# A ring of three PSUM banks for attention's turned tiles, one output bank copied by ScalarE, and another order of VectorE's rounds

## The reference

```python
for l in range(DEPTH):                       # DEPTH = 2
    proj = rms_norm(x, norm1[l]) @ w_in[l]
    o_a = causal_block_attention(q_a, k_a, v_a, 96 ** -0.5)            # "A"
    o_b = sliding_window_attention(q_b, k_b, v_b, swa_sinks[l], ...)   # "B"
    o_c = dsa_attention(q_c, k_c, v_c, qi, ki, c_w, top_k, ...)        # "C"
    o_d = causal_block_attention(..., log_f_cum=cum)                   # "D"
    x = x + concatenate([o_a, o_b, o_c, o_d]) @ w_out[l]
    x = x + square(relu(rms_norm(x, norm2[l]) @ w_up[l])) @ w_down[l]
```

## Time and profile before

| | |
|---|---|
| median of 3 runs | 1879.53 us (1877.53 to 1884.22) |
| the profiled execution | 1878.71 us, span 1876.9 us |
| mean granted TensorE clock | 0.985 |
| TensorE matmul, busy | 1815.8 us (97%) |
| VectorE, busy | 933.3 us (50%) |
| ScalarE, busy | 650.0 us (35%) |
| GpSimd, busy | 731.0 us (39%) |
| the chain that ended last | TensorE 81%, VectorE 8%, "issue" 6%, ScalarE 3%, GpSimd 2% |

### The profile page before, as it was taken

How to read it: one execution, slowest core, us unless ns; L and a number is a source line. 1 busy time by engine, 2 the same in 40 slices (tenths; PEclk the granted TensorE clock), 3 DMA queues, 4 the chain that set the end, 5 groups by cost and what they waited for, 6 DMA issues and landing times.

```text
span 1876.9 us, 22981 instructions
## 1 busy us (share of the span) xinstructions
PE 1815.8 (97%) x9055; PEld 1472.2 (78%) x9057; DVE 933.3 (50%) x1556; ACT 650.0 (35%) x1182; POOL 731.0 (39%) x328
## 2 busy tenths in 40 slices
PE   8999889999999999998999999999999999999997
PEld 7678558888888886785578888888788988888786
DVE  4668871614142336688725544628532124339374
ACT  4534452312221245344523121222434443443212
POOL 3232343444454433332534445445343333235342
PEclk9999899999999999998999999999899999999999
DMA  7225002222322333120014344342332222322211
GB/s 227 68 68 167 3 24 68 90 90 92 111 89 89 89 86 104 62 74 1 24 55 164 119 157 149 101 175 90 95 124 90 68 68 96 108 68 90 90 68 45
DMA packets 104448, 171.01 MB, mean 91 GB/s; under 512 B 21615, under 2 KB 39431, under 8 KB 103208
## 3 DMA queue, kind: packets, MB, share of 16 engines
q1 hardware_dynamic: 103320, 169.79, 27.6%
q10 hardware_dynamic: 1040, 0.00, 0.0%
HBM read 166.56 MB, written 7.93 MB: 93 GB/s over the span
## 4 chain that ended last, share of the span: by engine, by line
PE 81%; DVE 8%; issue 6%; ACT 3%; POOL 2%; DMA 0%; SPq 0%; DVEq 0%; POOLq 0%; ACTq 0%
PE G L2044 23%; PE G L2045 23%; PE G L2046 23%; POOL w_lo L1286 2%; PE S L2330 2%; DVE neg_max L1916 1%; PE S L1057 1%; DVE select L1880 1%; ACT prob L1513 1%; DVE work L1716 1%; PE S L1031 1%; PE G L2366 1%; DVE top L1715 1%; PE S L1042 1%; PE G L2347 1%
## 5 line engine op out<-in xcount | busy, mean ns | idle before, releaser
L1286 POOL TENSOR_TENSOR w_lo<-raw,w_hi 128x1024 fp32r<-128x1024 f32 (+2 forms) x268 | 661.0, 2487 | 989.4 <-ACT w_hi L1332 677.1
L2044 PE MATMUL G<-h_hi,w_hi 128*128 128x512 f32 x896 | 356.6, 398 | 4.0 <-POOL w_lo L1286 2.1
L1332 ACT ACTIVATE w_hi<-raw 128x2048 fp32r<-128x2048 f32 (+1 forms) x94 | 178.8, 1902 | 499.6 <-PE G L2046 499.6
L2046 PE MATMUL G<-h_hi,w_lo 128*128 128x512 f32 x896 | 350.4, 391 | 0.0
L2045 PE MATMUL G<-h_lo,w_hi 128*128 128x512 f32 x896 | 350.0, 391 | 0.0
L2044 PE MATMUL G<-w_hi,h_hi 128*128 128x512 f32 (+2 forms) x704 | 278.4, 395 | 5.7 <-issue 2.0
L2046 PE MATMUL G<-w_hi,h_lo 128*128 128x512 f32 (+2 forms) x704 | 268.7, 382 | 0.0
L2045 PE MATMUL G<-w_lo,h_hi 128*128 128x512 f32 (+2 forms) x704 | 268.3, 381 | 0.0
L2045 PE MATMUL G<-w_lo,u_hi 128*128 128x512 f32 x512 | 202.0, 394 | 0.0
L2044 PEld LDWEIGHTS G<-h_hi,w_hi 128*128 128x128 f32 x896 | 168.7, 188 | 42.3 <-issue 4.4
L2044 PE MATMUL G<-w_hi,u_hi 128*128 128x512 f32 x512 | 200.8, 392 | 0.0
(11 more groups left out here) (317 smaller groups left out, 2241.1 us busy)
## 6 DMA issues: line engine op xcount, KB each, us to landing
raw<-in_w_in_dram SPq DMA_DIRECT2D x40, 1024.0 KB, 5.2
raw<-in_w_up_dram SPq DMA_DIRECT2D x32, 1024.0 KB, 5.2
raw<-in_w_down_dram SPq DMA_DIRECT2D x32, 1024.0 KB, 5.0
raw<-in_w_out_dram SPq DMA_DIRECT2D x12, 1024.0 KB, 5.0
w_ada<-in_w_ada_dram SPq DMA_DIRECT2D x4, 3072.0 KB, 12.1
skew_scratch<-line_scratch SPq DMA_DIRECT2D x1, 4608.0 KB
raw<-in_w_in_dram SPq DMA_DIRECT2D x8, 512.0 KB, 4.4
raw<-in_w_in_dram SPq DMA_DIRECT2D x4, 832.0 KB, 6.7
```

Of the source, the lines that this page charges most:

```text
L1286: ins = pool.tensor_tensor(w_lo[:, c % SPLIT_SLOTS, part, 0:n], raw[:, c % RAW_SLOTS, part, 0:n], w_hi[:, c % SPLIT_SLOTS, part, 0:n].bitc ...
L1332: act.activation(w_hi[:, c % SPLIT_SLOTS, :, 0:n], raw[:, c % RAW_SLOTS, :, 0:n], ACT.Copy).then_inc(high_ready, 1)
L2044: pe.matmul(dst, a_hi, b_hi, start=first, stop=False)
L2046: return pe.matmul(dst, a_lo, b_hi, start=False, stop=last)
```

## The change

- The banks: turns go round banks 0, 1 and 2 of G; a turn waits for the turn three before it. All outputs go to bank 3, and an output waits until the one before it has been copied away.
- The takers: who copies a turn is now set by the unit or head (number n or e of it, even VectorE, odd ScalarE), no longer by the turn's number. The list TAKER keeps it, and the waits count in it.
- Output copies (L1944) go from VectorE to ScalarE, behind its copy of turned probabilities.
- Units of the next pair: one at step 0 of a pair, two at step 1, one at step 2; for C one at step 0 and one at step 1. Before, two at step 1 and two at step 2, for C both at step 1.
- VectorE's copy of a unit moves from the front of its step to the end of the step before, behind the rounds.
- Rounds: 36 instead of 30 are placed beside the projections, none of them in the last of those steps; 12 are left for the stage, two at steps 3, 7, 11 and 15 and one at 4, 8, 12 and 16.
- At the end, VectorE's splits get waits of their own for turns and outputs, and TensorE no longer waits for the output before the last ahead of the projection.

Cut to what is spoken of (left out are lines where only the bank's number changes, and VectorE's old `take_output`):

```diff
@@ -81,30 +81,51 @@
 def next_qk(i):
     p = ITEMS[min(i, NI - 1)][0] + 1
-    if i % TT not in (1, 2) or p == len(PAIRS):
+    if p == len(PAIRS):
         return p, ()
-    return p, range(2) if i % TT == 1 else range(2, qk_units(p))
+    return p, ((0,), (1, 2), (3,), ())[i % TT] if qk_units(p) == 4 else ((0,), (1,), (), ())[i % TT]
 def number_turns():
-    qk = {(0, n): n for n in range(qk_units(0))}
-    at, pt = qk_units(0), {}
+    qk, pt, taker = {}, {}, []
+    def add(places, key, who):
+        places[key] = len(taker)
+        taker.append(who)
+    for n in range(qk_units(0)):
+        add(qk, (0, n), n % 2)
     for i in range(NI + 1):
         p, units_now = next_qk(i)
         for n in units_now:
-            qk[p, n] = at
-            at += 1
+            add(qk, (p, n), n % 2)
         if i:
             for e in range(2):
-                pt[i - 1, e] = at
-                at += 1
-    return qk, pt, at
...
+QK_NO, PT_NO, TAKER = number_turns()
+LAYER_TURNS = len(TAKER)
+TURN_BANKS = 3
+def taken_by(who, no):
+    return TAKER[:no + 1].count(who)
+def turn_bank(no):
+    return no if no < 4 else (no - 4) % TURN_BANKS
+def bank_before(no):
+    return no - TURN_BANKS if no >= 4 + TURN_BANKS else turn_bank(no)
 MIX_ORDER = (0, 1, 2, 3, 4, 6, 7, 5)
@@ -179,9 +200,16 @@
 LAYER_SC = NB + NI
 LAYER_OV = NI
-EARLY_ROUNDS = 2 * ROUNDS
-EARLY_STEPS = side_steps(1, NS + 1)
-assert LAYER_TURNS % 2 == 0
+EARLY_ROUNDS = 9 * ROUNDS // 4
+EARLY_STEPS = side_steps(1, AT["M",]) - 1
+def late_rounds(i):
+    return {3: 2, 0: 1 if i else 0}.get(i % TT, 0)
+assert EARLY_ROUNDS + sum(late_rounds(i) for i in range(4 * TT + 2)) >= 3 * ROUNDS
...
@@ -1517,9 +1545,9 @@
                 def take_qk(p, units_now):
                     for n in units_now:
                         m, (what, _, at), no = head_width(p), qk_places(p)[n], QK_NO[p, n]
-                        if no % 2:
+                        if TAKER[no]:
                             act.wait_ge(turn_filled, turns + (no + 1))
-                            act.activation(qkT[0:m, p % 2, at, :], G[0:m, no if no < 4 else 1, :], ACT.Copy,
+                            act.activation(qkT[0:m, p % 2, at, :], G[0:m, turn_bank(no), :], ACT.Copy,
                                            scale=score_scale(p) if what == "q" else 1.0).then_inc(odd_drained, 1)
                 def take_probs(i):
@@ -1527,7 +1555,15 @@
                     act.wait_ge(turn_filled, turns + (PT_NO[i, 1] + 1))
                     if i >= 2:
                         act.wait_ge(o_filled, item0 + (i - 1))
-                    act.activation(probT[:, i % 2, 1, 0:width], G[:, 1, 0:width], ACT.Copy).then_inc(odd_drained, 1)
+                    act.activation(probT[:, i % 2, 1, 0:width], G[:, turn_bank(PT_NO[i, 1]), 0:width], ACT.Copy
+                                   ).then_inc(odd_drained, 1)
+                def take_output(i):
+                    p, qt = ITEMS[i]
+                    g, hp = PAIRS[p]
+                    q = slice(P * qt, P * qt + P)
+                    act.wait_ge(o_filled, item0 + (i + 1))
+                    act.activation(mixed(g, hp)[:, q], G[:, TT - 1, 0:P], ACT.Copy).then_inc(o_drained, 1)
                 def part_high(part):
                     c = MID_PIECE
@@ -1549,6 +1585,8 @@
                         exponentials(i + 1)
                     if i:
                         take_probs(i - 1)
+                    if i > 1:
+                        take_output(i - 2)
                     if i in MID_HIGH:
                         part_high(MID_HIGH[i])
                     for k in EARLY_SPLITS.get(i, ()):
@@ -1559,6 +1597,7 @@
                 act.wait_ge(o_drained, item0 + (5 * TT + PAIR_CREDIT))
                 for k in MIX_ORDER[HALF_K:KT - 1]:
                     high_mix(k)
+                take_output(NI - 1)
                 act.wait_ge(o_drained, item0 + (NI + PAIR_CREDIT))
                 high_mix(MIX_ORDER[KT - 1])
                 ahead(OUT_JOB, 0)
@@ -1719,16 +1758,16 @@
                     left = work[:, 0:P * (qt + 1)]
                     step.done(dve.tensor_scalar(chosen(qt), left, TAKEN * 0.9, NEG, ALU.is_gt, ALU.mult))
-                rounds = iter(range(EARLY_ROUNDS + ROUNDS))
+                rounds = iter(range(3 * ROUNDS))
                 round_steps = itertools.count()
                 def top_rounds(count=None):
                     if count is None:
                         k = next(round_steps)
+                        if k >= EARLY_STEPS:
+                            return
                         count = (k + 1) * EARLY_ROUNDS // EARLY_STEPS - k * EARLY_ROUNDS // EARLY_STEPS
-                        if k == EARLY_STEPS - 1:
-                            return
                     for r in itertools.islice(rounds, count):
                         top_round(1 + r // ROUNDS, r % ROUNDS)
                         if r % ROUNDS == ROUNDS - 1:
...
@@ -2289,29 +2324,27 @@
                 pe.wait_ge(bank_drained, unit + (TT * PROJ_JOBS - 3 + UNITS_CREDIT))
                 pe.wait_ge(even_taken, evens + (EVEN[AT["F",], "s"] + 1))
-                def turn_free(no):
-                    pe.wait_ge(odd_drained if no % 2 else even_drained, halves + (no // 2 + 2))
-                def turn_bank(no):
-                    return G[:, no if no < 4 else no % 2, :]
-                def turns_taken(no):
-                    pe.wait_ge(even_drained, halves + (no // 2 + 1 + PAIR_CREDIT))
-                    pe.wait_ge(odd_drained, halves + ((no + 1) // 2 + PAIR_CREDIT))
+                def unit_taken(no):
+                    who = TAKER[no]
+                    pe.wait_ge(odd_drained if who else even_drained,
+                               l * taken_by(who, LAYER_TURNS) + taken_by(who, no) + PAIR_CREDIT)
+                def units_taken(no):
+                    pe.wait_ge(even_drained, l * taken_by(0, LAYER_TURNS) + taken_by(0, no) + PAIR_CREDIT)
+                    pe.wait_ge(odd_drained, l * taken_by(1, LAYER_TURNS) + taken_by(1, no) + PAIR_CREDIT)
                 def give_qk(p, units_now):
                     for n in units_now:
                         (what, e, _), no = qk_places(p)[n], QK_NO[p, n]
                         if no >= 4:
-                            turn_free(no)
+                            unit_taken(bank_before(no))
                         elif no:
                             pe.wait_ge(bank_drained, unit + (TT * (PROJ_JOBS - 1) + no + 1 + UNITS_CREDIT))
                         for t in range(TT):
                             src = head_rows(p, what, e, t)
-                            ins = pe.transpose(turn_bank(no)[0:src.shape[1], P * t:P * t + P], src, ident)
+                            ins = pe.transpose(G[0:src.shape[1], turn_bank(no), P * t:P * t + P], src, ident)
                         ins.then_inc(turn_filled, 1)
                 def give_scores(i):
...
@@ -2358,11 +2391,11 @@
                     p = ITEMS[i][0]
                     tiles = key_tiles(i)
-                    turns_taken(PT_NO[i, 1])
-                    pe.wait_ge(o_drained, item0 + (i + 1))
+                    units_taken(PT_NO[i, 1])
+                    pe.wait_ge(o_drained, item0 + (i + PAIR_CREDIT))
                     for b, kb in enumerate(tiles):
-                        for e, dst in enumerate(output_bank(i)):
+                        for e, dst in enumerate(output_places()):
                             ins = pe.matmul(dst, values(p, e, kb), probT[:, i % 2, e, P * b:P * b + P],
                                             start=b == 0, stop=b == len(tiles) - 1)
                     ins.then_inc(o_filled, 1)
@@ -2384,8 +2417,6 @@
                         give_output(i - 2)
-                pe.wait_ge(o_drained, item0 + (NI - 1 + PAIR_CREDIT))
                 def last_bank_free(pos):
                     if pos == 3 * HALF_K - 1:
                         pe.wait_ge(o_drained, item0 + (NI + PAIR_CREDIT))
```

More of the change, by code:

```diff
@@ L1164, in mixed, with output_places @@
             return {"D": mixT_da, "A": mixT_da, "B": mixT_bc, "C": mixT_bc}[g][:, n + (2 if g in "AC" else 0), :]
-        def output_bank(i):
-            return [G[HD * e:HD * e + HD, 2 + i % 2, 0:P] for e in range(2)]
+        def output_places():
+            return [G[HD * e:HD * e + HD, TT - 1, 0:P] for e in range(2)]
         def select_at(qt):
@@ L1956, in _ @@
                         take_probs(i - 1)
[L1957 to L1960 removed]
+                    top_rounds(late_rounds(i))
+                    take_qk(*next_qk(i + 1))
                     if i + 1 < NI:
@@ L1963, in _ @@
                     if i == NI - 1:
+                        dve.wait_ge(turn_filled, turns + (PT_NO[NI - 2, 1] + 1))
                         split_mix(0, 2)
@@ L2126, in _ @@
                 unit, tr, item0, score0 = l * LAYER_UNITS, l * LAYER_TR, l * NI, l * LAYER_SC + NB
-                number, turns, halves = l * LAYER_PIECES, l * LAYER_TURNS, l * HALF_TURNS
+                number = l * LAYER_PIECES
```

33 lines of the change are left out of this document (14 added, 19 removed).

## The result

The changed kernel takes 1853.38 us (median of 4 runs, 1851.58 to 1854.34) against 1880.03 us (1877.53 to 1884.22) for the kernel before: a ratio of 0.9869, 95% interval 0.9851 to 0.9888. The profiled execution took 1854.13 us, its span is 1852.3 us, the mean granted clock 0.994; that is 24.6 us less in span than before. The forecast was 1856.5 us. One of the six executions of the version with two turn banks took 9632.1 us, for which no trace shows a reason; its median is given without it.

The account below looks back on a forecast made before the run. The two attention stages bound it, TensorE busy 77 to 81 of 90 to 92 us and waiting for banks and copies. Layers -13.9 and -12.2 make -26.1, hand-overs +3, so -23: 1856.5 us, range 1850 to 1872.

Parts of the forecast that it names:

- Start: First scores to the maxima of item 3 in each attention stage: -6.0 us in the first layer, -5.8 in the second.
- Periods: Each attention stage's four-item periods: 14.35, 14.8, 12.85, 12.4 us; first layer -3.85, -0.5, -1.05, -1.6, second layer's fourth -0.1.
- End: Last widest maxima to the output projection's first matmul: 17.38 to 15.7 us, -1.7 a layer, VectorE's splits beginning earlier.
- Hand-overs: Allowance for hand-overs that the pass leaves out: 48 items at 0.06 us give back 3 us.
- Rounds moved: Beside the projections, VectorE gets 8.5 us more a layer: +0.8 a layer, bounds 0 and 8.5 less 0.4.
- The wait that is added: One output bank: output(i-2) waits for ScalarE's copy of output(i-3); no cost beyond output(1)'s start at 3.2, plus 0.45 us a layer.
- The rival in which the single bank serialises: Slower rival: each output waits out the queued exponentials, mean 1.02 us, 48 cost 49 us, time 1905 us; chance 0.07.
- The clock falls all the same: Rival: short pauses still lower the clock in the stages, 4.6 us a layer, 9.2 in all, time 1865.7 us; chance 0.14.
- VectorE's three rounds keep the period: Rival: VectorE's queue at item 3 keeps periods at 15.3, 15.3, 13.9, 14.0 and 12.5; 6.8 us lost, 1863.3; chance 0.15.
- Moved rounds in full: Rival: the rounds moved beside the projections cost in full, 7.7 us more in each layer, time 1872 us; chance 0.07.

Follow-up runs that it names:

- the second experiment: The kernel before with only the new placing of rounds (36 beside the projections, 12 in the stage): 1890.99 us, ratio 1.0084.
- the first experiment: The changed kernel with the rounds placed as before (30 beside the projections, 18 in the stage): 1855.83 us, ratio 0.9891 against the kernel before.

## Why the prediction was right, point by point

**Parts and placing in one table.** Stages of layer 1 / layer 2 in us:

| | rounds as before | 36/12, two in a row | 36/12, singly |
|---|---|---|---|
| banks and order before | 92.08 / 90.32 | 94.17 / 94.13 | 87.70 / 87.67 |
| banks and order changed | 81.22 / 80.58 | 78.15 / 78.16 | 74.40 / 74.41 |

The ring, ScalarE's output copies, the unit copies at the end of the step and the three steps bring 13 to 16 us a stage in the last two columns and 10 to 11 in the first. The changed placing of the rounds is worth 2 to 3 us with the new banks and costs 2 to 4 with the old: the pair at step 3 is harmful in both rows, by 6.5 with the old banks and 3.75 with the new. I hadn't costed this coupling on its own. The clock is part of these numbers: its mean in the two stages is 0.89 and 0.94, 0.95 and 0.95, 0.94 and 0.94 in the first row, and 0.94 and 0.98, then 1.00 four times in the second. With the rounds singly, 8.7 of the 13.3 us between the rows are busy time of TensorE (77.43 against 68.78 us). How much of a gain is a shorter wait, and how much the clock that stays up behind it, these runs don't separate; only where both cells have 1.00, as with 78.15 and 74.40, is it the waits alone.

**Start**: right. 7.25 us in both layers, clock 1.00; the working had 7.25. Both parts of the change are in it: with the rounds back it is 11.28 with the same banks, with the rounds moved but the old banks and order 9.36, and with two turn banks and all else new 8.33.

**Periods**: the first 14.37 for a forecast of 14.35; the second 14.94 for 14.8; the third 13.00 for 12.85. The fourth is mis-sized: 12.87 for 12.4. Between 242.08 and 250.94 VectorE has no pause there, and behind the third round comes the mark of C's last tile:

```profile
249.26 0.43 DVE L1759 TENSOR_SCALAR select<-work 128x512 bf16<-128x512 f32 x1
...
249.81 0.94 DVE L1955 TENSOR_REDUCE neg_max<-S 128x2 f32<-128x768 f32 x1
```

My pass for that period named no mark. But with single rounds the same mark stands in the same place (245.01, behind the third round) and the period is 11.91. So the mark isn't enough to lengthen it; what the two kernels differ in is the pair of rounds at step 15. In the second layer, where the old period was 12.48, the changed kernel with 12.86 is slower than the old one there, for a forecast of 0.1 faster.

**End**: 15.72 for 15.7, right, and for the reason given: with the output copies back on VectorE it is 16.74.

**Hand-overs**: the allowance of 3 us had no row and was too large. Against the stages' forecast without it (27.7 us) 26.1 were won; the 1.6 that are missing are twice 0.47 in the fourth period, twice 0.14 in the second and twice 0.15 in the third. Those three periods get shorter with single rounds (13.69, 12.51, 11.91), so VectorE's queue is in them; no run shows a fee for each item, nor rules one out. The forecast lies 3.1 us above the median: 1.5 of it is the gain in the spans (24.6 for 23.1), 0.8 and 0.75 are how the two profiled executions lie to their medians, on opposite sides. That the total comes so near is partly luck. The moved rounds and the clock near 182 cost 3.2 us where 1.6 was forecast, and the last stretch, for which nothing was forecast, gave 1.7 back; that stretch moves by such a step between two executions of one kernel (last section).

**Rounds moved**: +0.8 a layer forecast, 2.17 and 1.02 measured. The wait near 160 came as forecast (1.0 worked out, 0.97 measured), the second layer has one of 1.0 too. The other 1.2 us of layer 1 are a fall of the clock which I hadn't foreseen (last section). The version with the units over two steps has the same code up to there and no fall: its first scores come at 188.19, 0.7 later than in the kernel before, as the +0.8 had it. The even spreading was the cause of the wait, not the number of rounds: with the same 36 placed by hand it is gone.

**The wait that is added**: right. The output waits once a period, about 1.1 us, where the old order had paused before turns. The rival in which the single bank serialises needed a mean wait of 0.54 us over 48 outputs; measured are 5.3 us over 24 in a stage, mean 0.22, and with a second output bank, which takes it away, the stage is 5.1 us longer, as that bank is missing for the turns. The Trainium skill, "PSUM — Partial Sum Buffer", "PSUM bank collisions raise a hardware error", says that two different engines may not be in the same 32 partitions of one bank at the same time; in different groups of 32 partitions they may. The prediction had it for the whole bank, which comes to the same here, as the output copy reads all 128 partitions. These runs can't test it, since the kernel's own waits keep them apart; what they show is that the separation costs little here, where ScalarE's output copy stands right behind its copy of turned probabilities.

**Rivals.** *The clock falls all the same*: not in the stage, where the clock is 1.00. *VectorE's three rounds keep the period*: wrong as I priced it (15.3), since the periods are 14.4 to 14.9, but right in kind. VectorE did keep the periods 0.5 to 1.3 us above what the same banks allow, 3.75 a stage, which comes on top of what the rival was priced at (3.4 a stage more than the forecast). In my working a pause of 0.8 us was all that reached TensorE, and the pauses for VectorE in the first period are that, 0.19 and 0.61 us. With single rounds the first two periods are 1.1 and 1.25 us shorter all the same (13.29 and 13.69 against 14.37 and 14.94), so the pauses alone understate what the pair of rounds costs. *Moved rounds in full*: no; beside the fall of the clock they cost about 1 us a layer of 8.5. Its price had a slip: 8.5 less 0.4 and less the 0.8 of the forecast is 7.3 a layer, which gives 1871 and not 1872. The reason given against it isn't contradicted. A round's replacement stayed at 0.68 us at most through 90 of them (view of one line: least, median, most ns):

```profile
L1755 DVE MATCH_REPLACE8 work<-top,work x90: 407/543/678, 88.8 to 898.7; 128x256 f32<-128x256 f32 x30, 128x384 f32<-128x384 f32 x30, 128x512 f32<-128x512 f32 x30
```

**The miss of the second experiment** has its root in this: I took the start's gain and the periods' as properties of the rounds' number in the stage. They depend on which copy stands behind the rounds in the step, and on how many turns later its bank is needed again. With three banks that slack is one turn longer.

## What to carry to other kernels

Where several engines share a few PSUM banks, count which tile's copy comes late and try the spare bank there: three for turned tiles and one for outputs was worth 5.1 us a stage of 83 here, against two and two. Filler work goes one piece at a time between copies that another engine waits for; the same twelve rounds cost 3.75 to 6.5 us more a stage in pairs. And where the periods are worked out one by one, don't add an allowance that no row supports; look at what else is queued on the engine that has no pauses.

## What the runs showed of the hardware

**The clock falls without a pause of TensorE.** In the changed kernel, first layer, windows of 2 us:

```profile
182.00:184.00 2.00, 2.00 (x9) 1.57 (x8) 1.90 (x8) 0.00 (x0) 0.00 (x0) 0.76 0.49 154
184.00:186.00 2.00, 2.00 (x7) 1.63 (x6) 1.22 (x3) 0.07 (x1) 0.00 (x0) 0.50 0.27 103
```

and TensorE's timeline:

```profile
179.48 2.29 PE L2235 MATMUL S<-log_f,masks 128*128 128x4 f32 x20
...
182.18 0.40 PE L2081 MATMUL G<-w_hi,h_lo 128*128 128x512 f32 x1
...
184.41 0.63 PE L2079 MATMUL G<-w_hi,h_hi 128*128 128x512 f32 x1
```

Matmuls of 0.40 us take 0.63 with TensorE busy throughout. Ahead of them stand twenty matmuls of four columns. Six at 0.43 us from start to start where 0.23 is usual make the 1.2 us. The kernel before has the same twenty at 178.59 and no fall at that place. Of the thirteen profiled executions eight have the fall and five don't: the kernel before, the first experiment, two turn banks, units over two steps, and early rounds by hand. The version with the units over two steps has the same code as the changed kernel up to there, with the twenty at 179.55 instead of 179.48. So the twenty aren't sufficient, the fall comes and goes without an edit ahead of it, and what decides is open.

**Falls at one place last differently.** A fall that begins between 1308 and 1352 us, during or close behind 32 matmuls of one column (L991 in the kernel before), is in ten of eleven executions read window by window. In the eleventh, with the units over two steps, the 32 stand at 1318.08 and the clock stays at 1.00 until 1328; it falls near 1330, behind a pause of 1.88 us. In the changed kernel it has windows of 0.50, 0.68, 0.74 and 0.83; with single rounds one of 0.57:

```profile
1320.00:1324.00 4.00, 4.00 (x8) 1.97 (x9) 3.43 (x13) 0.21 (x1) 0.00 (x0) 0.50 0.00 0
```

```profile
1312.00:1316.00 4.00, 4.00 (x11) 1.85 (x11) 3.33 (x14) 0.24 (x2) 0.00 (x0) 0.57 0.00 0
```

The last stretch takes 931.0, 932.7, 934.3 or 935.9 us over the thirteen profiled executions, steps of about 1.6, though of its code only the place of the last output copy and its waits changed. Two executions of the changed kernel differ by one such step (934.26 and 932.63), and by the reverse step between the layers (572.03 and 573.56). A difference of a few us in the whole is therefore read from the stage, where two executions agree to 0.01 us.

**Pauses and the clock.** In the changed kernel the clock stayed at 1.00 behind pauses of 1.10 us once a period, with two turn banks behind 1.21 us; behind one of 1.70 (first experiment) and 2.21 it fell. But the length of a pause doesn't decide alone. The second experiment has four long ones in its first stage, of 1.83, 1.83, 1.83 and 2.03 us. Behind the first (206.72) and the last (257.97) the clock falls to 0.50; behind the other two (225.94 and 242.79) it stays at 1.00. In windows, behind the first and then behind the second of them:

```profile
208.00:210.00 2.00, 2.00 (x7) 1.11 (x6) 1.00 (x3) 0.59 (x1) 1.04 (x1) 0.58 0.00 0
210.00:212.00 2.00, 2.00 (x12) 1.18 (x12) 1.00 (x2) 0.01 (x1) 0.00 (x0) 0.50 0.00 0
...
226.00:228.00 2.00, 1.70 (x10) 1.19 (x11) 1.93 (x6) 2.00 (x5) 0.25 (x1) 1.00 0.00 0
228.00:230.00 2.00, 2.00 (x23) 1.40 (x21) 1.28 (x3) 0.29 (x2) 2.00 (x2) 1.00 0.00 0
```

In the second layer of the first experiment a pause of 1.70 us (845.85) leaves the clock at 1.00, and it falls only behind a second one of 1.75 (851.63). Short pauses are no surer: three of 0.43, 0.56 and 0.61 us within 2.5 us of each other, with rounds kept singly in the old banks, were followed by a fall, and the same three in the second experiment were not. What decides is open.
